# A hybrid DeltaNet and sliding-window layer: the 16x16 diagonal blocks of each chunk's inverse by back substitution on GpSimd

## What is computed

```python
lower = jnp.where(strict, jnp.einsum('bhnid,bhnjd->bhnij', k_beta, kc) * decay, 0.0)
rhs = jnp.concatenate([v_beta, k_beta * jnp.exp(G)[..., None]], axis=-1)
sol = lax.linalg.triangular_solve(eye + lower, rhs, left_side=True, lower=True, unit_diagonal=True)
```

## Time and profile before

| | |
|---|---|
| median of 3 runs | 2222.03 us (2221.86 to 2222.96) |
| the profiled execution, time / span | 2220.89 us / 2219.1 us |
| TensorE (PE) busy | 2089.9 us, 94% |
| VectorE (DVE) busy | 1655.8 us, 75% |
| ScalarE (ACT) busy | 772.4 us, 35% |
| GpSimd (POOL) busy | 688.4 us, 31% |
| mean granted TensorE clock | 0.991 |

### The profile page before, as it was taken

How to read it: one execution, slowest core, us unless ns; L and a number is a source line. 1 busy time by engine, 2 the same in 40 slices (tenths; PEclk the granted TensorE clock), 3 DMA queues, 4 the chain that set the end, 5 groups by cost and what they waited for, 6 DMA issues and landing times.

```text
span 2219.1 us, 63767 instructions
## 1 busy us (share of the span) xinstructions
PE 2089.9 (94%) x26854; PEld 1700.3 (77%) x26854; DVE 1655.8 (75%) x4880; ACT 772.4 (35%) x2200; POOL 688.4 (31%) x1035
## 2 busy tenths in 40 slices
PE   0389999999999999999999999999999999999996
PEld 0378778878878877887887788788788778878874
DVE  5887777777777777777777777777777777777773
ACT  0533333333333333333333333333333333333332
POOL 0023333332323333332333323233322323332332
PEclk9999999999999999999999999999999999999997
DMA  7101000010000100000000000001100000001000
GB/s 296 65 22 32 2 31 32 32 31 32 31 2 31 32 31 32 32 29 4 31 32 31 31 31 17 17 32 32 32 31 31 6 27 32 32 31 32 22 2 29
DMA packets 26335, 75.37 MB, mean 34 GB/s; under 512 B 5129, under 2 KB 9538, under 8 KB 25026
## 3 DMA queue, kind: packets, MB, share of 16 engines
q1 hardware_dynamic: 26050, 71.29, 9.4%
HBM read 54.50 MB, written 16.78 MB: 32 GB/s over the span
## 4 chain that ended last, share of the span: by engine, by line
PE 82%; DVE 13%; ACT 2%; issue 1%; DMA 1%; SPq 0%; POOL 0%; POOLq 0%; DVEq 0%; ACTq 0%
PE bank L406 31%; PE bank L608 15%; PE bank L413 12%; PE bank L421 9%; DVE qkv L896 4%; PE bank L461 2%; PE bank L438 2%; PE bank L576 2%; PE bank L443 1%; PE bank L543 1%; DVE qkv L894 1%; PE bank L564 1%; DVE w_raw L1242 1%; PE bank L384 1%; DVE small L935 1%
## 5 line engine op out<-in xcount | busy, mean ns | idle before, releaser
L406 PE MATMUL bank<-xt_half,w_raw 128*128 128x128 f16 x15360 | 933.0, 219 | 54.5 <-DVE w_raw L1242 53.9
L406 PEld LDWEIGHTS bank<-xt_half,w_raw 128*128 128x128 f16 x15360 | 890.8, 98 | 66.9 <-DVE w_raw L1242 54.1
L896 DVE SCALAR_TENSOR_TENSOR qkv<-conv_in,cols,qkv 128x128 f32<-128x128 f32 x1152 | 436.4, 421 | 3.5
L413 PE MATMUL bank<-w_raw,xt_half 128*128 128x264 f16 (+1 forms) x1536 | 283.7, 328 | 1.0
L1301 POOL TENSOR_TENSOR cw<-mt,small 128x128 f32<-128x128 f32 x320 | 135.1, 446 | 344.7 <-PE bank L438 321.1
L413 PEld LDWEIGHTS bank<-w_raw,xt_half 128*128 128x128 f16 x1536 | 144.3, 99 | 84.3 <-DVE w_raw L911 8.3
L715 ACT ACTIVATE work<-bank 128x128 f32<-128x128 f32 x160 | 44.4, 277 | 372.3 <-PE bank L443 372.3
L608 PE MATMUL bank<-w_o,inv_t 128*128 128x512 f16 x768 | 171.0, 379 | 2.1 <-DVE inv_t L1175 2.1
L608 PE MATMUL bank<-w_o,out_b_half 128*128 128x512 f16 x768 | 171.0, 379 | 0.0
L675 ACT ACTIVATE tanh_c<-qkv 128x512 f32<-128x512 f32 x96 | 60.5, 630 | 281.5 <-DVE qkv L896 281.5
L1349 POOL TENSOR_TENSOR small<-small 128x1 f32<-128x1 f32 x32 | 6.2, 193 | 435.2 <-ACT work L815 435.2
(11 more groups left out here) (215 smaller groups left out, 3575.4 us busy)
## 6 DMA issues: line engine op xcount, KB each, us to landing
x_in<-in_x_dram SPq DMA_DIRECT2D x32, 512.0 KB, 4.7
y_out<-in_x_dram SPq DMA_DIRECT2D x32, 512.0 KB, 4.0
out_dram<-y_out SPq DMA_DIRECT2D x32, 512.0 KB, 2.9
w_raw<-in_w_in_dram SPq DMA_DIRECT2D x8, 1024.0 KB, 13.5
w_o<-in_w_out_dram SPq DMA_DIRECT2D x8, 512.0 KB, 13.4
w_raw<-in_w_in_dram SPq DMA_DIRECT2D x8, 384.0 KB, 12.4
w_raw<-in_w_in_dram SPq DMA_DIRECT2D x8, 256.0 KB, 13.2
rot_tab<-in_rotary_dram SPq DMA_DIRECT2D x32, 64.0 KB, 4.2
```

What stands on the lines that cost most here:

```text
L406: last = mm(dst[:, 128 * b:128 * b + 128], w_half[:, c, ws, col:col + 128], xt_half[:, xs, c, :], start=(c == 0 and ws + xs == 0), stop=(c ...
L413: last = mm(dst[:, 0:n_col], xt_half[:, xs, c, :], w_half[:, c, ws, col:col + n_col], start=(c == 0 and ws + xs == 0), stop=(c == NC - 1 a ...
L896: last = v.scalar_tensor_tensor(dst, conv_in[:, b, i:i + TOK], tap, dst, ALU.mult, ALU.add)
```

## The change

Levels 0 to 3 of the inverse go. `BASE = 4`, `BLOCK = 16`: the 16x16 diagonal blocks are inverted directly, by back substitution along the free axis on GpSimd. VectorE masks `mt` to its diagonal blocks (128x512) and folds them to 128x64 (`m_near`). SyncE stores that in DRAM (128 x 256 bytes) and loads it back so that every partition holds its whole block (128 x 4 KB, into `y_out`, which is free then). GpSimd then runs 1 + 30 linked operations, each waiting for the one before, and two more that spread the result into `t_even(4)` and `t_odd(4)`. TensorE takes up at level 4. The residual load into `y_out` now waits until GpSimd is through. GpSimd's multiplication of the softmax moves to ScalarE (8 operations). TensorE's pieces, 26 as before, are placed anew. One `tensor_scalar` of the k norms becomes a `scalar_tensor_tensor`.

```diff
 # SyncE, per step, after the loads of x and of the rotary table
+                    done(sp, near_ready, m)
+                    sp.dma_start(near_dram, m_near.rearrange("p h n -> p (h n)")).then_inc(near_stored, 16)
+                    sp.wait_ge(near_stored, (m + 1) * 16)
                     ...
                         sp.wait_ge(stored, m * 16)
+                    sp.dma_start(y_out[:, 0:BLOCK * 4 * BLOCK],
+                                 near_dram.rearrange("(b j) n -> b (j n)", j=BLOCK).unsqueeze(1).broadcast_to(
+                                     [128 // BLOCK, BLOCK, 4 * BLOCK * BLOCK])).then_inc(block_loaded, 16)
+                    done(sp, to_ready, m)
                     sp.dma_start(y_out[:, :], x[0, bass.ds(m * TOK, TOK), :]).then_inc(res_loaded, 16)
 # TensorE
-                done(pe, u0_ready, m)
-                done(pe, u0_blank, m)
                 done(pe, q_t_ready, m)
-                for h in range(4):
-                    last = nc.tensor.transpose(heads(2)[:, h, :], inv_u[:, h, :], ident)
-                last.then_inc(u0_turned, 1)
...
-                fill(1)
...
                 last.then_inc(scores_ready, 1)
-                fill(1)
-                level_p(1)
-                fill(1)
-                level_t(1)
-                fill(1)
-                level_p(2)
+                fill(2)
...
                 per_head(7, k4, state, ks_ready)
-                fill(1)
-                level_t(2)
-                fill(1)
-                level_p(3)
+                fill(4)
...
                 last.then_inc(soft_turned, 1)
-                fill(1)
-                level_t(3)
-                fill(1)
+                fill(2)
 # ScalarE: copy_u(1) to copy_u(3) and the packing of level 0 are gone; after small_fill
+                    done(act, rsum_ready, m)
+                    for hh in range(8):
+                        last = f(soft[:, hh, :], soft[:, hh, :], ACT.Identity, scale=row_sum[:, hh:hh + 1])
+                    last.then_inc(soft_ready, 1)
 # VectorE: couple and update of levels 1 to 3 are gone
-                    v.tensor_scalar(norms[:, 0:4], norms[:, 0:4], 0.25, EPS, ALU.mult, ALU.add).then_inc(k_norms_ready, 1)
+                    v.scalar_tensor_tensor(norms[:, 0:4], norms[:, 0:4], 0.25, eps4, ALU.mult, ALU.add).then_inc(
+                        k_norms_ready, 1)
...
-                    v.tensor_tensor(halves(prod, 0, 1), halves(mt[:, :, :], 0, 1),
-                                    mask_halves(masks[:, 0, :], 0, 1), ALU.mult).then_inc(c0_ready, 1)
...
+                    v.tensor_tensor(prod, mt[:, :, :], over_heads(same_base, 4), ALU.mult).then_inc(near_made, 1)
+                    done(dve, near_masked, m)
+                    v.tensor_reduce(m_near, prod.rearrange("p h (b n) -> p h n b", n=BLOCK), AX_X, ALU.add).then_inc(
+                        near_made, 1)
 # GpSimd: the blanking L1307, pack_m(1) to pack_m(3) and the softmax product are gone
                     pack_m(4)
                     pack_m(5)
+                    invert_base(m)
...
+                linked(g.tensor_tensor(base_inv[:, :, :], over_heads(spot, 4), ..., ALU.mult))
+                pool.wait_ge(block_loaded, (m + 1) * 16)
+                for k in range(BLOCK - 1, 0, -1):
+                    linked(g.tensor_tensor(x_prod[:, :, 0:k], m_block[:, 0:k, :, k].rearrange("p j h -> p h j"),
+                                           base_inv[:, :, k:k + 1].broadcast_to([128, 4, k]), ALU.mult))
+                    linked(g.tensor_tensor(base_inv[:, :, 0:k], base_inv[:, :, 0:k], x_prod[:, :, 0:k], ALU.subtract))
+                for which, dst in ((0, t_even(BASE)), (1, t_odd(BASE))):
+                    g.tensor_tensor(dst.rearrange("p (h q n) -> p h q n", h=4, q=pairs), ..., ALU.mult).then_inc(base_made, 1)
```

More of the change, by code:

```diff
@@ L150, in build @@
         y_out = sb("y_out", [128, D])
+        m_block = y_out[:, 0:BLOCK * 4 * BLOCK].rearrange("p (j h n) -> p j h n", j=BLOCK, h=4)
         def w_out_half(c):
@@ L161, in build @@
         ident, upper, neg = c32[:, 0, :], c32[:, 1, :], c32[:, 2, :]
+        same_base = masks[:, BASE, :]
+        spot = masks[:, 0, 0:2 * BLOCK].bitcast(F32)
+        fold = [None] * BASE + [masks[:, 1, 0:64], masks[:, 1, 64:128]]
+        near = masks[:, 2:4, :].rearrange("p l n -> p (l n)").bitcast(F32)
+        m_near, x_prod = near[:, 0:64].rearrange("p (h n) -> p h n", h=4), near[:, 64:128].rearrange("p (h n) -> p h n", h=4)
+        base_inv = sb("base_inv", [128, 4, BLOCK])
+        near_dram = nc.dram_tensor("near_scratch", (128, 4 * BLOCK), F32, kind="Internal").ap()
         rows = x_in[0:57, 0:128]
@@ L164, in build @@
         conv_taps = cols[:, 0:48]
-        small = sb("small", [128, 201])
+        small = sb("small", [128, 205])
         def cut(at, n):
@@ L192, in build @@
         one = cut(200, 1)
+        eps4 = cut(201, 4)
         const_loaded, x_loaded, rot_loaded, res_loaded, stored, wo_loaded, pw_loaded = (
@@ L228, in build @@
             {lv: Nth(s, hi - lo + 1, lv - lo) for lv in range(lo, hi + 1)} for s, lo, hi in (
-                (sem("p_turn"), 1, 6), (sem("p_ready"), 1, 6),
-                (sem("tp_turn"), 1, 5), (sem("t_turned"), 1, 6), (sem("t_ready"), 1, 5),
-                (sem("u_ready"), 1, 6), (sem("t_moved"), 1, 5), (sem("m_odd_ready"), 1, 5)))
+                (sem("p_turn"), BASE, 6), (sem("p_ready"), BASE, 6),
+                (sem("tp_turn"), BASE, 5), (sem("t_turned"), BASE, 6), (sem("t_ready"), BASE, 5),
+                (sem("u_ready"), BASE, 6), (sem("t_moved"), BASE, 5), (sem("m_odd_ready"), BASE, 5)))
         mask_turned, mask_link = sem("mask_turned"), sem("mask_link")
-        c0_ready, u0_ready, u0_blank, u0_turned, t0_ready = (
-            sem(n) for n in ("c0_ready", "u0_ready", "u0_blank", "u0_turned", "t0_ready"))
+        near_made, near_stored, block_loaded, base_made = (
+            sem(n) for n in ("near_made", "near_stored", "block_loaded", "base_made"))
+        near_masked, near_ready = (Nth(near_made, 2, i) for i in range(2))
+        te_ready, to_ready = (Nth(base_made, BASE_LINKS + 2, BASE_LINKS + i) for i in range(2))
         up_turn, inverse_ready, k_sq_ready, k_sq_used = (
@@ L267, in over_heads, with over_heads2 @@
             return ap.unsqueeze(1).broadcast_to([128, h, ap.shape[1]])
+        def over_heads2(ap):
+            return ap.unsqueeze(1).broadcast_to([128, 4, ap.shape[1], ap.shape[2]])
         def halves(ap, lv, which):
@@ L425, in level_p @@
                 def level_p(lv):
-                    if lv == 1:
-                        done(pe, t0_ready, m)
+                    if lv == BASE:
+                        done(pe, te_ready, m)
                     else:
@@ L741, in step @@
                     f(k_win[:, :, 64:192], heads(3)[:, 0:2, :], ACT.Copy).then_inc(k_win_ready, 1)
[L742 to L749, removed]
                 if proj:
@@ L844, in _ @@
             dve.wait_ge(mask_link, LEVELS - 1)
-            v.tensor_tensor(masks[:, 1:LEVELS - 1, 0:64], masks[:, 1:LEVELS - 1, 0:64],
-                            masks[:, 1:LEVELS - 1, 64:128], ALU.add)
+            for lv in range(BASE, LEVELS - 1):
+                v.tensor_tensor(fold[lv], masks[:, lv, 0:64], masks[:, lv, 64:128], ALU.add)
+            v.tensor_reduce(spot, ident.rearrange("p (b n) -> p n b", n=BLOCK), AX_X, ALU.add).then_inc(mask_link, 1)
+            v.memset(inv_u[64:128, :, 0:64], 0.0)
             v.memset(halo[:, :, :], 0.0)
@@ L1353, in step, with invert_base, linked @@
                     g.tensor_tensor(y_rs, y_arg, power[:, 0:1], ALU.pow).then_inc(y_rs_ready, 1)
+            def invert_base(m):
+                count = 0
+                def linked(ins):
+                    nonlocal count
+                    count += 1
+                    ins.then_inc(base_made, 1)
+                    pool.wait_ge(base_made, m * (BASE_LINKS + 2) + count)
+                linked(g.tensor_tensor(base_inv[:, :, :], over_heads(spot, 4), one.broadcast_to([128, BLOCK]).unsqueeze(1).broadcast_to([128, 4, BLOCK]), ALU.mult))
+                pool.wait_ge(block_loaded, (m + 1) * 16)
[3 more added lines that the diff above has]
+                    linked(g.tensor_tensor(base_inv[:, :, 0:k], base_inv[:, :, 0:k], x_prod[:, :, 0:k], ALU.subtract))
+                assert count == BASE_LINKS
+                pairs = 64 // (2 * BLOCK)
+                for which, dst in ((0, t_even(BASE)), (1, t_odd(BASE))):
+                    g.tensor_tensor(dst.rearrange("p (h q n) -> p h q n", h=4, q=pairs),
+                                    base_inv[:, :, :].unsqueeze(2).broadcast_to([128, 4, pairs, BLOCK]),
+                                    over_heads2(fold[BASE].rearrange("p (q s n) -> p q s n", s=2, n=BLOCK)[:, :, which, :]),
+                                    ALU.mult).then_inc(base_made, 1)
             def post(m):
```

34 lines of the change are left out of this document (9 added, 25 removed).

## The result

The changed kernel takes **2247.11 us** (2236.49 to 2250.49, four runs), the kernel before 2221.95 on the same chip (2221.66 to 2222.96): a ratio of 1.0104, interval 1.0071 to 1.0138. It is slower by 1.0%, where 2203 us, 0.9% less than before, was forecast. The time lies in the range that was given, the sign is not the one forecast. The profiled execution took 2247.0 us, its span is 2245.2 and its mean granted clock 0.970, against 0.991 before.

A forecast was written before the change was run, and what follows sets the result against it. TensorE was taken as the bound; relieved of 3.21 us, it would wait some 2 us for the GpSimd chain, leaving rounds of 64.35, 0.72 less. Over 31 steps -22.3, +2 in step 32: 2203 us, range 2140 to 2262.

The forecast's parts named there:

- the load: DMA bringing the blocks from DRAM into y_out, 512 KB: 4.4 us (3.6 to 5.5), taken from the residual load's 4.0.
- what leaves TensorE: Removed transposes, three level_p and three level_t, 2.61 us, plus 0.6 for six switches: 3.21 us a step.
- A predicted small term: GpSimd's rotations meet VectorE's last convolution taps, whose end TensorE awaits at L468: 0.4 us (0 to 1.0).
- T: When te_ready lets TensorE start level 4: 1145.8, where TensorE would arrive at 1143.91; a round of 63.75 us.
- Rival 3: Block load on 8 of 16 DMA engines, source outer dimension 8: T 0.7 us later, 2221 us, no change; chance 0.12.
- the store's term: Store of the folded blocks to DRAM, 32 KB: 2.1 us (1.7 to 2.9), from an output store with data at 377 GB/s.
- The undisturbed sum: GpSimd's 30 linked operations without port conflicts: 10.0 us, plus 0.3 for strided reads.
- The port term: Delay of GpSimd's links by VectorE operations on the port both share: 2.2 us (0.8 to 4.0).
- Rival 2: Shared port decides: VectorE's 16 operations cost 0.25 each, 4.0 us, round 66.15, time 2258 us, slower; chance 0.26.
- the fold: VectorE's folding of the masked blocks ahead of the store, over 512 elements: 0.7 us.
- rival 4: Clock falls after a wait of some 2 us at level 4 each step: time 2233 us; chance 0.05.
- Step 32: Step where nothing fills TensorE: level_p(4) starts at 2183.4 instead of 2181.45, so +2 us.

The follow-up runs named there:

- the kernel with one block: Changed kernel whose block load brings the first diagonal block to all 128 partitions (source outer dimension 128, not 8; other inverses wrong): 2138.31 us, ratio 0.9624.
- the set-wait kernel: Changed kernel with back substitution on constants, not waiting for the block load, and 25 added links, so level 4 waits 2.65 us: 2234.73 us, ratio 1.0055.
- The runs with a set wait: Changed kernel with links on constants plus 25 added links (wait 2.65 us, 2234.73 us) or 28 (wait 3.65 us, 2296.28 us).
- the longer cover: Changed kernel with two of TensorE's 26 pieces moved from behind level 4 to ahead of it: 2143.67 us, ratio 0.9649.

## Where the prediction was right, and where it failed

The forecast was a gain of 0.72 us a step, and the kernel lost about 0.5. The term that turned the sign is the clock, which the sum put at nothing; behind it stands the load, which was put too short.

**Right: what leaves TensorE, and what then bounds a step.** 3.21 was said, 3.30 measured. The chain through GpSimd ends the cover, TensorE waits for it in every step and nowhere else of weight. L1019 keeps its 1.83. A predicted small term stands too: L494 waits up to 0.61 where 0.4 was given.

**Near in sum, wrong in two terms: T.** In the kernel before, the gram of the step of the earlier trace rows starts at 1120.94:

```profile
1120.94 2.00 PE L421 MATMUL bank<-qkv 128*128 128x128 f32 x16
```

Counted from there, T was given as 24.9 (1145.8 - 1120.94) and is 25.52. That it came so near is luck, since two errors nearly cancel.
- *The load, 4.4 given, 6.83 measured.* The step that failed is "The nearest row is the residual load, as large and to the same place". That row had the size and the place, but not the shape. Rival 3 had the shape and the right mechanism, eight engines. It failed in its price, 0.7 more. By its own numbers that was too little: 2.8 us on eight engines stand against 1.4 at 377 GB/s, the figure of the store's term, and not against 2.1. (Its time is off as well: the round falls by 0.02, which gives 2223 and not 2221. And the forecast itself adds up to 2201.7, not 2203.) Measured were 115 to 152 GB/s, with each packet at 0.25 us where the residual load has 0.21; why isn't shown. The prediction did name this as what would refute it: "if the load takes over 5.5". The Trainium skill (DMA: Bandwidth & Descriptors, on why a DMA increments its semaphore by 16) holds here: share 0.5 with an outer dimension of 8, 0.9 with 128.
- *GpSimd's links with the port, 12.5 given (10.3 and 2.2), 10.20 measured.* The undisturbed sum was right within 0.2. The port term was wrong: the links took 10.10 to 10.33 in every step, whatever VectorE ran, so GpSimd paid 0.2 at most here (up to 0.4 in the kernel with one block, where they took 10.10 to 10.50). VectorE paid more: four L902 beside the links take 1.56 and 1.33, against 1.13 alone. The row that misled was L1367 at 0.44, a single operation; it doesn't carry over to this chain of short ones. Rival 2 (0.26) falls with it.
- Two small ones: the fold took 1.03 for 0.7 (that its stride of 64 bytes is the reason isn't shown), and with it 5.76 to the issue of the store stands where 5.36 was given. The store itself took 2.25 for 2.1.

The four add up to +0.4 + 0.15 + 2.4 - 2.3 = some +0.66 a step.

**Wrong: the clock.** This step turned the sign. With a wait of 2.65 and the clock kept, the set-wait kernel has rounds of 64.93, which is 61.77 + 2.65 + 0.51 (the last for L494 and `to_ready`). So with T as it was and the clock kept, the changed kernel's round would be 61.77 + 2.55 + 0.51, 64.83; over 31 rounds that is some 7 us less than 65.07. Measured were 65.57. The missing 0.74 a step, 23 us, goes with the clock, which fell behind the wait in two thirds of the steps. It was rival 4, priced at 1.0 a step (close) with a chance of 0.05 (far off). The reason against it was that "in step 32 TensorE was half idle all around, here it is full". The runs with a set wait refute that: one idle stretch of 2.65 us in a round otherwise full costs 0.26 us on average, one of 3.65 costs 1.23. They don't give the changed kernel's 0.74, though. With the same mean wait, but between 1.59 and 3.88, it has 21 of 30 rounds at 0.98 or less, and the set wait of 2.65 has nine. What makes the difference, the unevenness or something else, is open.

**Sum.** From the gram of step 1 to that of step 32, 31 rounds, the changed kernel needs 65.65 each and the kernel before 65.05: +18.6 where -22.3 was said. Of these 41 us the longer chain gives 20 and the clock 23, the first mixing step some 2; some 6 come off, since the relief and the small terms were each 0.09 a step better than given; about 1 is left over. Step 32 costs +4.9 where +2 was said: 24.7 from gram to level 4 against 20.8 before, and 1.0 more behind it. The remaining 2.6 us lie ahead of step 1, in the set-up. There the runs differ by up to 3.4 us (143.5 to 146.8 at that gram), also where that part is the same; why is open.

**Still open.** A single load of the eight blocks that uses 16 engines was not tried, nor one from GpSimd's queue. Nor was the softmax factor on ScalarE tried alone; TensorE waits for L769 twice in the whole kernel. What decides whether a wait of 1.6 to 3.4 us costs the clock isn't known.

## What to carry to other kernels

When work leaves the bounding engine for a chain elsewhere, compare the chain's length with the cover left ahead of its consumer, and move independent work into that cover in the same edit: two pieces moved made a loss of 1.0% a gain of 3.5%. For a DMA, look at the outer dimension of both sides before taking its time from a row of equal size. And price a recurring wait on TensorE at more than its length: here one of 2.55 us on average cost 0.74 more.

## What the runs showed that was not expected

- An otherwise full TensorE loses clock to one short wait a round: none lost without a wait (61.77 in every round) or with waits of up to 0.94 (the longer cover), 0.26 us a round at a wait of 2.65, 1.23 at 3.65. A single wait of 1.59 has cost it, one of 3.37 has not. In the step shown, two pieces behind the wait take 2.77 and 2.53 in place of 1.50.
- A 512 KB load whose source has an outer dimension of 8 ran at a DMA share of one half and 115 to 152 GB/s, one of 128 at up to 0.9 and 377. Split into eight loads of 16 rows it was hardly faster (6.39 for 6.83), with packets as slow (0.24 and 0.25 us) and 0.45 us for each issue.
- Thirty linked GpSimd operations of 4 to 60 elements were hardly slowed by VectorE (10.10 to 10.33 in all steps); VectorE was slowed by them, by 0.43 and 0.20 in four taps.
- An operation taken off the port they share frees only what the next one doesn't wait for: 1.7 us of stall removed, 1.05 of it back two operations later.
